# Paged attention in a decoder step: a cached page in one quarter of the partitions, four keys to a partition, and a sample's queries copied in runs of 1 KB

## What is computed

```python
past_c = cache_kv_latent[page_table].reshape(DB, past_len, KV_LORA)   # (8, 2048, 512)
past_kr = cache_k_rope[page_table].reshape(DB, past_len, QK_ROPE)     # (8, 2048, 64)

def sample_attention(q_lat, q_rope, past_c, past_kr, c, kr):
    s_past = latent_scores(q_lat, q_rope, past_c, past_kr)
    s_new = latent_scores(q_lat, q_rope, c, kr)                       # + causal mask
    p = softmax(concat([s_past, s_new], -1))
    return einsum('bhqk,bkc->bqhc', p[..., :P], past_c) + einsum('bhqk,bkc->bqhc', p[..., P:], c)
```

## Time and profile before

| | us |
|---|---|
| median of 3 runs | 1835.25 |
| lowest, highest | 1833.23, 1840.73 |
| the profiled execution | 1836.92 |
| its span | 1835.1 |

### The profile page before, as it was taken

The page is one execution under the profiler, slowest core; times in us unless marked ns, Lnnn a source line. Parts: engine busy times, 40 slices in busy tenths (PEclk is TensorE's granted clock), DMA queues, the critical chain, the costliest instruction groups (busy, mean ns, idle before and its releaser), DMA issues.

```text
span 1835.1 us, 39585 instructions
## 1 busy us (share of the span) xinstructions
PE 1688.3 (92%) x15798; PEld 1560.5 (85%) x15798; DVE 929.4 (51%) x2134; ACT 681.5 (37%) x1296; POOL 966.4 (53%) x795
## 2 busy tenths in 40 slices
PE   7998899998999999999898587788989999999998
PEld 6997799998999999989676445555989999999988
DVE  5897799944323556672555444554161222222283
ACT  5565444454444444532233101112342222322342
POOL 4994799966899975753210000002555445555652
PEclk9999999999999999999999899789999999999999
DMA  7322455534455441323003356664512222222201
GB/s 209 106 82 60 131 162 171 170 132 138 131 169 161 161 138 32 99 69 123 1 1 98 100 155 181 172 178 137 187 47 90 71 92 92 81 79 69 93 24 53
DMA packets 204723, 203.92 MB, mean 111 GB/s; under 512 B 53801, under 2 KB 158851, under 8 KB 204562
## 3 DMA queue, kind: packets, MB, share of 16 engines
q1 hardware_dynamic: 179726, 194.28, 34.0%
q10 hardware_dynamic: 24836, 7.41, 1.7%
HBM read 192.14 MB, written 4.79 MB: 107 GB/s over the span
## 4 chain that ended last, share of the span: by engine, by line
PE 65%; DVE 10%; POOL 9%; SPq 6%; issue 4%; ACT 3%; DMA 2%; ACTq 2%; POOLq 0%; DVEq 0%
PE bank L2550 19%; PE bank L2552 19%; PE bank L2551 19%; POOL WL L1522 4%; SPq L516 2%; ACTq L1400 2%; SPq L508 2%; SPq L502 2%; PE bank L3089 2%; POOL R L1585 1%; PE bank L3056 1%; POOL root L1585 1%; POOL WL L1520 1%; PE bank L3127 1%; DVE bank L1803 1%
## 5 line engine op out<-in xcount | busy, mean ns | idle before, releaser
L1522 POOL TENSOR_TENSOR WL<-RAW,WH 128x1024 fp32r<-128x1024 f32 (+3 forms) x279 | 574.3, 2066 | 254.5 <-ACT WH L832 252.9
L2550 PE MATMUL bank<-AH,WH 128*128 128x288 f32 x2080 | 626.1, 301 | 30.0 <-DVE AL L1775 13.2
L2551 PE MATMUL bank<-AL,WH 128*128 128x288 f32 x2080 | 616.8, 297 | 0.0
L2552 PE MATMUL bank<-AH,WL 128*128 128x288 f32 x2080 | 616.5, 296 | 0.0
L2550 PEld LDWEIGHTS bank<-AH,WH 128*128 128x128 f32 x2080 | 394.3, 190 | 41.9 <-DVE AL L1775 16.6
L2551 PEld LDWEIGHTS bank<-AL,WH 128*128 128x128 f32 x2080 | 394.6, 190 | 0.7
L2552 PEld LDWEIGHTS bank<-AH,WL 128*128 128x128 f32 x2080 | 394.3, 190 | 0.0
L832 ACT ACTIVATE WH<-RAW 128x1024 fp32r<-128x1024 f32 (+1 forms) x281 | 291.8, 1045 | 263.2 <-PE bank L2552 263.0
L2550 PE MATMUL bank<-BH,WH 128*128 128x288 f32 (+1 forms) x1120 | 336.2, 300 | 14.6 <-DVE S L1824 4.9
L1520 POOL TENSOR_TENSOR WL<-RAW,WH 128x256 fp32r<-128x256 f32 (+2 forms) x135 | 119.2, 903 | 432.4 <-PE bank L3127 306.1
L2552 PE MATMUL bank<-BH,WL 128*128 128x288 f32 (+1 forms) x1120 | 332.9, 297 | 0.0
(11 more groups left out here) (308 smaller groups left out, 2088.7 us busy)
## 6 DMA issues: line engine op xcount, KB each, us to landing
RAW<-in_w_up SPq DMA_DIRECT2D x48, 1024.0 KB, 5.4
RAW<-in_w_down SPq DMA_DIRECT2D x48, 1024.0 KB, 5.0
RAW<-in_cache_kv_latent SPq DMA_DIRECT2D x64, 256.0 KB, 3.4
WIDE<-in_cache_kv_latent SPq DMA_DIRECT2D x64, 256.0 KB, 3.4
RAW<-in_conv_pw SPq DMA_DIRECT2D x16, 512.0 KB, 6.9
RAW<-in_conv_pw SPq DMA_DIRECT2D x8, 1024.0 KB, 5.0
RAW<-in_ple_gate SPq DMA_DIRECT2D x8, 1024.0 KB, 4.9
S<-S ACTq DMA_DIRECT2D x136, 32.0 KB
```

The lines of the kernel that those rows point to most:

```text
L1522: nc.gpsimd.tensor_tensor(dst, src, hi, ALU.subtract).then_inc(lo_done, 1)
L2550: nc.tensor.matmul(out, wh, xh, start=first, stop=False)
L2551: nc.tensor.matmul(out, wh, xl, start=False, stop=False)
L2552: return nc.tensor.matmul(out, wl, xh, start=False, stop=last)
```

## The change

Three things go together. A page goes into 32 partitions in place of 128: page q of a half lies in partitions 32q to 32q + 31, with keys 4r to 4r + 3 one after another in partition 32q + r, latents (8 KB to a row) and ropes (1 KB to a row) alike. Number, queue, semaphores and total bytes of the loads stay. The place has the same shape, and DVE's transposes are unchanged; a column group k is now the k-th key of each partition. QLAT is stored sample by sample, so that a sample's four tiles are one run of 1 KB in a partition. And Q4 keeps its 16 latent blocks in the order n = 4m + c, so that a copy writes one run of 1 KB too; `scores` maps n back to the block b = 4c + m of TURN.

```diff
@@ L317
-        QLAT = S[:, 2880:4928].rearrange("p (c q) -> p c q", c=4)
+        QLAT = S[:, 2880:4928].rearrange("p (s c q) -> p s c q", s=NS, c=4)
@@ load_latents, load_ropes
                 for q in range(4):
-                    sp.dma_start(dst[:, :, q * CL:(q + 1) * CL],
-                                 io["cache_kv_latent"].rearrange("n p c -> p n c")[:, bass.ds(pages[q], 1)])\
+                    sp.dma_start(dst[32 * q:32 * q + 32],
+                                 io["cache_kv_latent"].rearrange("n (p k) c -> p n (k c)", k=4)[:, bass.ds(pages[q], 1)])\
                         .then_inc(half_landed(u, s)[0], 16)
...
-                    sp.dma_start(dst[:, :, q * DR:(q + 1) * DR],
-                                 io["cache_k_rope"].rearrange("n p c -> p n c")[:, bass.ds(pages[q], 1)])\
+                    sp.dma_start(dst[32 * q:32 * q + 32],
+                                 io["cache_k_rope"].rearrange("n (p k) c -> p n (k c)", k=4)[:, bass.ds(pages[q], 1)])\
@@ queries
                 for m in range(4):
                     for a in range(4):
-                        act.dma_start(Q4[i % 2][32 * a:32 * a + 32, 0:16].rearrange("p (c m) q -> p m c q", m=4)[:, m],
-                                      QLAT[32 * m:32 * m + 32, :, 64 * i:64 * i + 64]).then_inc(q4_in, 16)
+                        act.dma_start(Q4[i % 2][32 * a:32 * a + 32, 4 * m:4 * m + 4], QLAT[32 * m:32 * m + 32, i]).then_inc(q4_in, 16)
@@ head_latent (DVE)
-                nc.vector.tensor_copy(QLAT.rearrange("p c (s h t) -> p c s h t", s=NS, h=NH)[:, :, :, hd, :],
+                nc.vector.tensor_copy(QLAT.rearrange("p s c (h t) -> p c s h t", h=NH)[:, :, :, hd, :],
@@ new_keys
-                    nc.tensor.matmul(dst, QLAT[:, c, 64 * i:64 * i + 64], CS[:, c, :], start=c == 0, stop=False)
+                    nc.tensor.matmul(dst, QLAT[:, i, c, :], CS[:, c, :], start=c == 0, stop=False)
@@ scores
-                for b in range(18):
+                for n in range(18):
+                    b = 4 * (n % 4) + n // 4 if n < 16 else n
                     for a in range(4):
                         rows32 = slice(32 * a, 32 * a + 32)
                         for g in range(2):
-                            ins = nc.tensor.matmul(score_bank(u, a)[64 * g:64 * g + 64], Q4[u // 2 % 2][rows32, b, :],
-                                                   TURN[u % 2][rows32, b, P * g:P * g + P], start=b == 0, stop=b == 17)
+                            ins = nc.tensor.matmul(score_bank(u, a)[64 * g:64 * g + 64], Q4[u // 2 % 2][rows32, n, :],
+                                                   TURN[u % 2][rows32, b, P * g:P * g + P], start=n == 0, stop=n == 17)
```

## The result

The changed kernel takes 1855.33 us at the median (1849.44 to 1859.38) against 1838.9 for the kernel before beside it. The ratio is 1.0096, with a 95% interval of 1.0071 to 1.0121: slower by some 16 us by the medians (18 by the ratio), where 11 less were forecast. The profiled execution took 1858.36 us with a span of 1856.5, 21.4 more than the span before.

A forecast was written before the change was run, and what follows sets the result against it. Attention loops of SP (28.7), ACT (28.4) and TensorE (28.5 us), with stalls, gave 31.4 per sample. Falling to 29.7 over seven saves 11.9, less 0.7 for later landings: 1825.7, at the median 1824; range 1809 to 1858.

The forecast's parts named there:

- The load costs SP nothing more to issue: SP's page loads, 32 per sample: bounds 0 to +0.16 us each, 0 to +5.1 us per sample; taken as 0.
- SP pays more: Rival, chance 0.20: each SP page load into fewer partitions costs +0.158 us, + 17 us in all, 1852.
- The query copies cost nothing less: ACT's query copies, 16 of 18 per sample: bounds 0 to -0.31 us each; taken as 0.
- The stalls go with the number of rows: SP and ACT queues: fewer rows remove the stalls, 3.0 us per sample on SP and 1.7 on ACT.
- Nothing moves: Rival, chance 0.15: the queue stalls come from something else than the rows; 1835, give or take 5.
- Later landings move the stage once, by 0.7 us: Page loads in the samples' attention: three units of slack, so later landing costs 0.7 us once, not each time.
- with the sample's page table: SP's loop: reading page numbers between units takes 7.7 us with the sample's page table, within 28.7 us per sample.
- TensorE's standstills: TensorE inside the scores: 4.1 us per sample, no releaser named; the forecast is wrong if they grow.
- Half of the rate: Rival, chance 0.15: page loads into 32 partitions run at half rate, delaying pages and query copies; + 10.5 us, 1846.
- above 0.7: Sign of the half-rate rival: the DMA share of the samples' attention rises above 0.7 at the same bytes.
- 76% of a period, so the bytes still don't bind: Half-rate rival: a sample's two units and queries need 23.9 us of the DMA engines at 222 GB/s.
- dearer issues: Upper end of the range, 1858: SP's dearer page loads with 1 us of stalls left per sample (+ 7).

The follow-up runs named there:

- e7: Changed kernel with each page in 64 neighbouring partitions (rows of 4 KB latents, 512 bytes ropes) in place of 32: ratio 1.0149.
- e3: Changed kernel with each page spread over every fourth partition in place of 32 neighbours, rows still 8 KB: ratio 1.0129.
- e2: Changed kernel with the old page loads (128 partitions, 2 KB rows), leaving the queries' part of the change alone: ratio 0.9990, 1834.8 us.
- e11: Changed kernel with the page table fetched one sample ahead and only half of each latents row loaded in samples three to eight: ratio 0.9953.
- e5: Changed kernel with the page table fetched one sample ahead into a second buffer: ratio 1.0122.
- e4: Changed kernel, still 32 neighbouring partitions to a page, but four latents rows of 2 KB per partition in place of one of 8 KB: ratio 1.0092.
- e12: Kernel before with the page table fetched one sample ahead and nothing else: ratio 0.9972.
- e6: Changed kernel with the old page loads and the page table fetched one sample ahead: ratio 0.9951, 1828.1 us.
- e9: Kernel before with each sample's page table fetched twice, one fetch behind the other: ratio 1.0060.
- e1_loads: Kernel before with the change's page loads alone (32 neighbouring partitions, 8 KB rows), queries kept and copied as before: ratio 1.0098.

## Why the prediction was wrong, step by step

*The load costs SP nothing more to issue.* Right: 316 ns for 333. The rival "SP pays more" did not happen in this change, though e7 and e3 show that a price of this size (0.15 us for a bound of 0.16) is real for other sets of partitions.

*The query copies cost nothing less.* Right in the time: e2 stands at 0.999.

*The stalls go with the number of rows.* Wrong, and this was the whole of the forecast gain. In the changed kernel SP's 52 groups of four between first and eighth mark still sum to 17.3 us above 52 x 1.81, 2.5 per sample, for 2.9 before counted in the same way. The queue with a quarter of the rows stalls nearly as before, and e11 with half of the bytes stalls as e5 does with all of them (3.5 in both). The fifteen copies on ACT (start us, us, what) still take 10.6 to 11.2 us in the seven later samples for 9.6 in the first:

```profile
1021.28 9.60 ACTq L1400 DMA_DIRECT2D S<-S  x15
...
1084.82 11.13 ACTq L1400 DMA_DIRECT2D S<-S  x15
...
1249.15 10.62 ACTq L1400 DMA_DIRECT2D S<-S  x15
```

What the stalls come from, no run here settles. The sentence against the forecast was there, in "Nothing moves": a stall in the first group of a burst with little in flight. It deserved more than 0.15.

*Later landings move the stage once, by 0.7 us.* Wrong, and this was the loss: the forecast put the bytes behind a slower landing at nothing beyond these 0.7 us. The step looked for who waits for the pages and found three units of slack, which held: SP waited for no buffer, and a landing of pages stands in the chain between second and eighth mark once, with 5.8 us (1219.81) for 4.3 before (1176.00). It didn't look for who shares the queues with the pages. Two do: the fetch of the page table, which stood in the prediction's own sum only as the 7.7 us gap "with the sample's page table", and TensorE's standstills, whose growth it named as a thing that would upset it but didn't price. Priced from the queue: 10.6 us of transfer for 7.8 to 8.1 of issue leaves 2.5 to 2.8 us behind each unit, on SP's serial path once per sample, and 2.6 is what the gap grew by. The standstills grew by 2.7 us per sample. The two are not to be added: e5 takes the first away and the time stays.

*Half of the rate.* This rival, at 0.15, is what happened, and its signs came: a share of 0.75 for "above 0.7", 220 GB/s for the 222 worked out from the earlier trace rows, and last copies (S<-R) that landed as late as 6.57 us after their issue, as this one does in the chain of waits after:

```profile
1261.29 6.57 DMA S<-R
```

By the Trainium skill's SBUF — State Buffer, "Door 1: The DMA port swizzle", partitions 0 to 31 reach 8 of the 16 ports. e3 and e4 agree with it for writes, the part that no row before had shown: by the same section's map every fourth partition reaches all 16 ports, and e3 moves 310 GB/s. It puts partitions 0 to 63 on 8 ports too; e7, with 64 neighbours, is low at 234 GB/s, which agrees. The rival's time, 1846, was 9 us short. It had the delay on the query copies, and let the stage pay by ACT's loop. SP's path and TensorE's paid instead, side by side. "76% of a period, so the bytes still don't bind" was true as a mean, and the mean was the wrong thing: the engines were behind in each burst, and what waited behind the burst was on the path.

The range held the time (1809 to 1858), by luck: its upper end came from dearer issues, which did not happen (and by its own sum, 1852 + 7, it is 1859). The forecast's sign was wrong.

## What to carry to other kernels

Where a transfer is to get slower, or to go into a few neighbouring partitions, compare the rate at which a queue issues bytes with the rate at which they land, burst by burst, and list every small transfer and every instruction stream that uses the same engines behind the burst; a mean share with room in it says nothing of them. A small fetch whose value the issuing queue waits for belongs ahead of the burst: that was worth 0.3% (e12) and 0.4% (e6 against e2) here. And when two loops are equally long, taking one cause away shows nothing (e5) although it is real (e9): take away what both have in common (e11).

## What the runs showed of the hardware

- GB/s divided by the DMA share, over seven samples: loads into 32 neighbouring partitions 212 to 224 (265 in e11, whose engines are busy for 43%), into 64 neighbours 234, into all 128 286 to 298, and into every fourth partition 310 to 312 with 8 KB rows.
- The issue of a page load on SP: 316 to 317 ns into 32 neighbours (rows of 8, 4 or 2 KB alike), 333 into 128, 469 into 64, 472 into every fourth.
- TensorE stood still for up to 5.2 us inside a run of matmuls (e1_loads, 1188.24 to 1193.46, DMA share 1.05), with no semaphore to wait for. Such standstills come at multiples of about 128 matmuls, that is 256 instructions with their weight loads, and one packet of instructions, 16 KB, goes to 256 of TensorE's instructions.
- A table of 64 bytes fetched by an issuing queue landed 1.2 to 2.7 us after its issue behind a burst at full rate and 3.7 to 4.9 behind one at the lower rate.
